# Gate and up products of a SwiGLU MLP with weight columns on the partitions, so that the product needs no transposes

## The reference, cut to what matters

```
h2 = rmsnorm(x, norm_g[l, 1]) * (1.0 + sc2) + sh2
gate, up = jnp.split(h2 @ w_gate_up[l], 2, axis=-1)      # 2048 -> 2 x 5632
x = x + g2 * ((jax.nn.silu(gate) * up) @ w_down[l])      # 5632 -> 2048
```

## Time and profile before

| | |
|---|---|
| median of the runs | 2326.41 us |
| the profiled execution | 2323.81 us, its span 2322.0 us |
| matmuls, each with a load | 9820 |
| of them gate and up products | 4224 (2 layers x 22 chunks x 4 tiles x 24) |
| of them transposes of the MLP | 176 (44 turns x 4) |
| TensorE clock granted, mean | 0.975 of full speed |

### The profile page before, as it was taken

How to read it: one execution, slowest core, us unless ns; L and a number is a source line. 1 busy time by engine, 2 the same in 40 slices (tenths; PEclk the granted TensorE clock), 3 DMA queues, 4 the chain that set the end, 5 groups by cost and what they waited for, 6 DMA issues and landing times.

```text
span 2322.0 us, 26203 instructions
## 1 busy us (share of the span) xinstructions
PE 2158.4 (93%) x9820; PEld 1766.4 (76%) x9820; DVE 1664.1 (72%) x2386; ACT 979.2 (42%) x1400; POOL 202.9 (9%) x388
## 2 busy tenths in 40 slices
PE   2678998689999999999998999998999999999999
PEld 1467786468888888888886877787888888888887
DVE  6977999768867888788786688565975545555555
ACT  3333454154434444443444444445443444444343
POOL 3201111101101111111110011000100000000000
PEclk9889999889999999999998999999999999999999
DMA  9968778748858888888874675443975555555554
GB/s 404 390 241 310 264 273 309 281 154 326 326 191 311 316 321 322 313 317 316 322 304 165 238 294 188 179 166 144 343 280 199 181 196 186 198 182 198 186 195 145
DMA packets 110492, 590.70 MB, mean 254 GB/s; under 512 B 12448, under 2 KB 13088, under 8 KB 63904
## 3 DMA queue, kind: packets, MB, share of 16 engines
q1 hardware_dynamic: 54640, 386.55, 45.6%
q0 software_dynamic: 55296, 201.35, 23.1%
q10 hardware_dynamic: 432, 1.13, 0.1%
HBM read 586.88 MB, written 2.10 MB: 254 GB/s over the span
## 4 chain that ended last, share of the span: by engine, by line
PE 72%; DVE 12%; DMA 9%; issue 5%; ACT 2%; POOL 0%; DVEq 0%; ACTq 0%; POOLq 0%
PE ps L459 22%; PE ps L464 22%; PE ps L463 22%; DMA ada<-w_ada 8%; DVE ada L1202 3%; DVE w_lo L1178 3%; PE ps L762 1%; DMA qT<-w_ada 1%; PE ps L570 1%; PE ps L486 1%; PE ps L659 1%; PE ps L702 1%; PE ps L627 0%; ACT bufa L927 0%; DVE qT L1202 0%
## 5 line engine op out<-in xcount | busy, mean ns | idle before, releaser
L1178 DVE TENSOR_TENSOR w_lo<-raw,w_hi 128x1024 fp32r<-128x1024 f32 x704 | 846.5, 1223 | 366.3 <-ACT w_hi L858 366.0
L858 ACT ACTIVATE w_hi<-raw 128x1024 fp32r<-128x1024 f32 x704 | 734.8, 1057 | 716.0 <-PE ps L464 675.4
L459 PE MATMUL ps<-w_hi,h_hi 128*128 128x512 f32 x1920 | 776.8, 405 | 34.6 <-DVE w_lo L1178 21.6
L464 PE MATMUL ps<-w_hi,h_lo 128*128 128x512 f32 x1920 | 757.6, 395 | 0.0
L463 PE MATMUL ps<-w_lo,h_hi 128*128 128x512 f32 x1920 | 757.6, 395 | 0.0
L459 PEld LDWEIGHTS ps<-w_hi,h_hi 128*128 128x128 f32 x1920 | 367.0, 191 | 118.5 <-issue 33.1
L463 PEld LDWEIGHTS ps<-w_lo,h_hi 128*128 128x128 f32 x1920 | 366.6, 191 | 79.3 <-issue 5.3
L464 PEld LDWEIGHTS ps<-w_hi,h_lo 128*128 128x128 f32 x1920 | 365.9, 191 | 78.4
L459 PE MATMUL ps<-w_hi,a_hi 128*128 128x512 f32 x896 | 356.7, 398 | 5.4 <-issue 2.8
L464 PE MATMUL ps<-w_hi,a_lo 128*128 128x512 f32 x896 | 349.5, 390 | 0.0
L463 PE MATMUL ps<-w_lo,a_hi 128*128 128x512 f32 x896 | 349.1, 390 | 0.0
(11 more groups left out here) (164 smaller groups left out, 1071.3 us busy)
## 6 DMA issues: line engine op xcount, KB each, us to landing
raw<-stream SPq DMA_DIRECT2D x360, 1024.0 KB, 4.9
ada<-w_ada POOLq DMA_DIRECT2D x338, 512.0 KB, 5.7
qT<-w_ada POOLq DMA_DIRECT2D x12, 512.0 KB, 12.0
gate<-w_ada POOLq DMA_DIRECT2D x10, 512.0 KB, 12.5
raw<-stream SPq DMA_DIRECT2D x4, 896.0 KB, 6.7
kT<-w_ada POOLq DMA_DIRECT2D x6, 512.0 KB, 12.0
val<-w_ada POOLq DMA_DIRECT2D x6, 512.0 KB, 10.9
uc<-w_ada POOLq DMA_DIRECT2D x6, 512.0 KB, 12.0
```

What stands on the lines that cost most here:

```text
L459: mm = pe.matmul(bank[:], xh, whi[s][:, k, :], start=begin, stop=False)
L464: mm = pe.matmul(bank[:], xl, whi[s][:, k, :], start=False, stop=end)
L858: act.activation(whi[h % 4][:].rearrange("p k c -> p (k c)"), raw[t % 4][:, a * 1024:(a + 1) * 1024], ACT.Copy).then_inc(hi_ready.sem, 1)
L1178: dve.tensor_tensor(wlo[h % 4][:].rearrange("p k c -> p (k c)"), raw[t % 4][:, a * 1024:(a + 1) * 1024], whi[h % 4][:].rearrange("p k c -> ...
```

## The change

The gate and up products use a new function, `tile_turned`. Here 128 weight columns are loaded and all 256 tokens stream past, so a bank has inner columns on its partitions: bank 0 of a chunk's pair holds the 256 gate columns (two blocks of 128, tokens side by side), bank 1 the up columns. A half tile is 2 sides x 2 blocks x 2 k-steps x 3 matmuls: 24 matmuls with 256 columns, 48 for a tile. silu is one activation of 512 elements per partition, the product with up one operation of 512, and their result already stands as `a_hi` and `a_lo` want it. The transposes, `turned_at` and the MLP's use of banks 5 and 6 go; the down products wait on a new semaphore `ff_ready`. All other products keep `tile`.

```diff
@@ new, beside tile
+            def tile_turned(t, banks, rows, first, last, between=None):
+                h = half_of(t)
+                for a in range(2):
+                    s = (h + a) % 4
+                    pe.wait_ge(hi_ready.sem, hi_ready.at(here, h + a + 1))
+                    pe.wait_ge(lo_ready.sem, lo_ready.at(here, h + a + 1))
+                    for side in range(2):
+                        bank, free, value = banks[side]
+                        if first and a == 0:
+                            pe.wait_ge(free, value)
+                        for i in range(2):
+                            cols = slice((2 * side + i) * P, (2 * side + i + 1) * P)
+                            to = bank[:, i * T:(i + 1) * T]
+                            for k in range(2):
+                                xh, xl = rows[2 * a + k]
...
+                                mm = pe.matmul(to, whi[s][:, k, cols], xh, start=begin, stop=False)
...
+                                pe.matmul(to, whi[s][:, k, cols], xl, start=False, stop=False)
+                                mm = pe.matmul(to, wlo[s][:, k, cols], xh, start=False, stop=end)
+                        mm.then_inc(gemm_done.sem, 1)
+                    if a == 0 and between is not None:
+                        between()
@@ PE, mlp_part
-                def turn(k):
-                    pe.wait_ge(bank_of(k).free.sem, bank_of(k).free.at(here, use(k)))
-                    for tok in range(TOKS):
-                        b = chunk_bank(c0 + k, tok)
-                        pe.wait_ge(chunk_free[b].sem, chunk_free[b].at(here, (c0 + k) // 2 + 1))
-                    for i in range(2):
-                        for tok in range(TOKS):
-                            at = (i * TOKS + tok) * P
-                            src = tok * 256 + i * P
-                            mm = pe.transpose(bank_of(k).tile[:, at:at + P], bufb[:, k % 2, src:src + P], ident)
-                    mm.then_inc(bank_of(k).full.sem, 1)
...
-                    for k in turned_at(o, ups, m):
-                        turn(k)
...
-                    norm(2, t0, (chunk(c0), chunk(c0 + 1)))
+                    norm(2, t0, (chunk(c0), chunk(c0 + 1)), tile_turned)
                 for m in range(8 if o == 0 else 0, 4 * ups):
-                    tile(t0 + m, chunk(c0 + m // 4), h_rows(m % 4), m % 4 == 0, m % 4 == 3, lambda m=m: middle(m))
+                    tile_turned(t0 + m, chunk(c0 + m // 4), h_rows(m % 4), m % 4 == 0, m % 4 == 3,
+                                lambda m=m: middle(m))
...
                     if n == 0:
-                        for k in (2 * g, 2 * g + 1):
-                            pe.wait_ge(bank_of(k).free.sem, bank_of(k).free.at(here, use(k) + 1))
+                        pe.wait_ge(ff_ready.sem, ff_ready.at(here, 6 * o + 2 * g + 2))
@@ ACT, mlp_part
-                        act.activation(bufa[:, k % 2, tok * 256:(tok + 1) * 256],
-                                       ps[chunk_bank(c0 + k, tok)][:, 0:256], ACT.Silu)\
-                            .then_inc(silu_done.sem, 1)
+                    act.activation(bufa[:, k % 2, :], ps[b][:], ACT.Silu).then_inc(chunk_free[b].sem, 1)
...
-                    act.activation(a_hi[:, 2 * k:2 * k + 2, :].rearrange("p k t -> p (k t)"), bank.tile[:],
+                    act.activation(a_hi[:, 2 * k:2 * k + 2, :].rearrange("p k t -> p (k t)"), bufb[:, k % 2, :],
                                    ACT.Copy).then_inc(ff_hi.sem, 1)
@@ DVE, mlp_part
-                        dve.tensor_tensor(bufb[:, k % 2, tok * 256:(tok + 1) * 256],
-                                          bufa[:, k % 2, tok * 256:(tok + 1) * 256], ps[b][:, 256:512],
-                                          ALU.mult).then_inc(chunk_free[b].sem, 1)
+                    dve.tensor_tensor(bufb[:, k % 2, :], bufa[:, k % 2, :], ps[b][:], ALU.mult)\
+                        .then_inc(chunk_free[b].sem, 1)
...
-                    dve.tensor_tensor(a_lo[:, 2 * k:2 * k + 2, :].rearrange("p k t -> p (k t)"), bank.tile[:],
-                                      hi, ALU.subtract).then_inc(bank.free.sem, 1)
+                    dve.tensor_tensor(a_lo[:, 2 * k:2 * k + 2, :].rearrange("p k t -> p (k t)"), bufb[:, k % 2, :],
+                                      hi, ALU.subtract).then_inc(ff_ready.sem, 1)
```

More of the change, by code:

```diff
@@ L87, in done_before @@
     return [m // 4 - 1] if m % 4 == 0 and 1 <= m // 4 <= ups else []
-def turned_at(o, ups, m):
-    return [] if o == 0 and m == 7 else [0, 1] if o == 0 and m == 8 else done_before(o, ups, m)
 def ordered(events):
@@ L121 @@
     + [(50 + j, 0, f"norm2 {j}") for j in range(1, 8, 2)])
-A_MLP, B_MLP = len(A_USE), len(B_USE)
 ST_NORM1, ST_KV, ST_Q0, ST_KCMP, ST_Q1, ST_NORM2, STAGES = 0, 8, 12, 14, 15, 17, 25
@@ L355, in build @@
         squared = count("squared", 16, 0, 8)
-        silu_done = count("silu_done", 12 * PARTS + 2 * LAST_UP, 12)
-        ff_hi = count("ff_hi", 6 * PARTS + LAST_UP, 6)
+        ff_hi, ff_ready = count("ff_hi", 6 * PARTS + LAST_UP, 6), count("ff_ready", 6 * PARTS + LAST_UP, 6)
         cond_ready = count("cond_ready")
@@ L467, in tile @@
                         between()
+            def tile_turned(t, banks, rows, first, last, between=None):
[13 more added lines that the diff above has]
+                                xh, xl = rows[2 * a + k]
+                                begin = first and a == 0 and k == 0 and i == 0
+                                end = last and a == 1 and k == 1 and i == 1
+                                mm = pe.matmul(to, whi[s][:, k, cols], xh, start=begin, stop=False)
+                                if a == 1 and side == 0 and i == 0 and k == 0:
+                                    mm.then_inc(raw_free[t % 4].sem, 1)
+                                pe.matmul(to, whi[s][:, k, cols], xl, start=False, stop=False)
[3 more added lines that the diff above has]
+                        between()
             def h_rows(g):
@@ L488, in norm_turn, with norm @@
                 mm.then_inc(bank.full.sem, 1)
-            def norm(which, t0, chunks):
+            def norm(which, t0, chunks, multiply):
                 split = 8 * (which - 1)
@@ L509, in norm @@
                             pe.wait_ge(h_ready.sem, h_ready.at(here, split + 2 * g + 1))
-                        tile(t, banks, h_rows(g), g == 0, g == 3, between)
+                        multiply(t, banks, h_rows(g), g == 0, g == 3, between)
             def stage_turn(bank, use, st, tok, n, stage=None):
@@ L789, in _ @@
                 here.layer = layer
-                norm(1, T_KV, (chunk(C_KV), chunk(C_KV + 1), window_chunk()))
+                norm(1, T_KV, (chunk(C_KV), chunk(C_KV + 1), window_chunk()), tile)
                 for i, t in enumerate((*T_Q0, *T_Q1)):
@@ L1092, in silu @@
                         act.wait_ge(x_updated.sem, x_updated.at(here, 16 + 8 * o))
[L1093 to L1098, removed]
-                        act.activation(bufa[:, k % 2, tok * 256:(tok + 1) * 256],
-                                       ps[chunk_bank(c0 + k, tok)][:, 0:256], ACT.Silu)\
-                            .then_inc(silu_done.sem, 1)
+                    if k >= 2:
+                        b = chunk_bank(c0 + k, 1)
+                        act.wait_ge(chunk_free[b].sem, chunk_free[b].at(here, (c0 + k - 2) // 2 + 1))
+                    b = chunk_bank(c0 + k, 0)
+                    chunk_done(t0 + (6 if o == 0 and k == 0 else 4 * k + 3), 0)
+                    act.activation(bufa[:, k % 2, :], ps[b][:], ACT.Silu).then_inc(chunk_free[b].sem, 1)
                 def rows(k):
-                    bank, base = (bank_a, A_MLP) if k % 2 == 0 else (bank_b, B_MLP)
-                    act.wait_ge(bank.full.sem, bank.full.at(here, base + 3 * o + k // 2 + 1))
-                    act.activation(a_hi[:, 2 * k:2 * k + 2, :].rearrange("p k t -> p (k t)"), bank.tile[:],
+                    b = chunk_bank(c0 + k, 1)
+                    act.wait_ge(chunk_free[b].sem, chunk_free[b].at(here, (c0 + k) // 2 + 1))
+                    act.activation(a_hi[:, 2 * k:2 * k + 2, :].rearrange("p k t -> p (k t)"), bufb[:, k % 2, :],
                                    ACT.Copy).then_inc(ff_hi.sem, 1)
@@ L1118, in mlp_part @@
                         split_hi(t0 + m + 1, 1)
-                    for k in turned_at(o, ups, m):
+                    for k in done_before(o, ups, m):
                         rows(k)
```

21 lines of the change are left out of this document (8 added, 13 removed).

## The result

The changed kernel takes 2354.07 us (median of four runs, 2348.30 to 2356.98) against 2326.44 us of the kernel before. The ratio is 1.0118, 95% interval 1.0096 to 1.0139: it is slower by some 28 us. The forecast was 2310 us, faster.

A forecast was written before the change was run, and what follows sets the result against it. The MLP was taken as bound by PE's stream of matmuls: +5.7 us for the new pace and -22.2 us for turns and waits gave -16.5 us, so 2310 us, faster, with a range of 2300 to 2339 us.

The forecast's parts named there:

- I take x = 114.0: Gate and up products: x, the pace of a 256-column matmul, is 114.0 ns; 8448 of them add 5.7 us.
- half of p is 113.3 ns: MLP on PE: p, the pace of a 512-column matmul, is 226.7 ns, so one of 256 takes 113.3 ns.
- rival 2: Gate and up products: load and stream no longer absorb each other's delays; 117.7 ns, 2341 us, slower above 116.5 ns; chance 0.22.
- The nearest row: Gate logits, 256 moving tokens and 24 loaded columns: mean 116.0 ns, steady stretch 114.0, taken as the new matmuls' pace.
- The floor by the load: PE in the MLP: a load of 128 columns needs about 111.4 ns, so it fits below 113.3 by some 2 ns.
- Rival 1: Gate and up products: pace is the gate logits' mean, 116.0 ns; +0.3 us, about 2327 us, no change; chance 0.14.
- Rival 3: Gate and up products: loads not hidden behind the stream, or by their 188 ns row; +600 us or more; chance 0.02.
- the turn: MLP on PE: each of the 44 turns removed costs 0.48 us, 21.1 us in all.
- No wait for `ff_ready`: Down products, tightest in the last part: DVE finishes `a_lo` in time, 0.8 us left, so the new wait costs nothing.
- the worth of all turns: MLP on PE: 21.1 us for the turns and 1.1 us of PE's waits go, together 22.2 us.
- what is late next is again PE itself: MLP stretches: with turns gone PE still bounds, since no other engine fills them; the 22.2 us count in full.
- rival 4: PE meets another wait, DVE's low parts in part 0 or `ff_ready`; most of 22.2 us returns, about 2325 us; chance 0.04.

The follow-up runs named there:

- experiment 1: Changed kernel with tile in place of tile_turned in the MLP: tokens loaded, 512 weight columns stream, no turns made; 2311.56 us, ratio 0.9931 to the kernel before.
- experiment 2: Changed kernel with weights loaded but 512 columns of h streaming past each load, half as many matmuls; 2311.38 us, ratio 0.9923 to the kernel before.

## Why the prediction was wrong

**The step that failed** is the pace of the new matmul, "I take x = 114.0". It measured 120.0, which is 8448 x 6.0 = +50.7 us. The whole forecast missed by 44 us (-16.5 forecast, +27.6 by the medians), so this one term more than explains it. Of its three grounds two were wrong.
- The frame: "half of p is 113.3 ns" was taken as the stream's own pace at 256 columns. The 226.7 ns of the earlier trace rows hold 512 columns and one fixed part, and halving halves the fixed part too. Columns at 2.4 GHz take 213.3 of them; the 13.3 left over was in sight. Read as fixed, it gives 106.7 + 13.3 = 120.0, the number measured. One width can't tell a rate from a rate with a constant, so both should have been ends. My upper end was 117.7, and even so the range stopped at 2339 us, 2 below rival 2's own 2341.
- The nearest row: the gate logits match in the moving columns but load 24. The runs with 64, 96 and 128 loaded go at 113.3, 116.0 and 120.0, so at 256 the load's size matters, and the row was near in the wrong dimension. "Loading as such doesn't slow the stream" rested on it and is wrong at 256.
- The floor by the load, 111.4 ns, was right (111.6 with fp32r), and beside the point.

**Rival 2** had the side right (slower, "above x = 116.5") and the size too small (117.7 ns, 2341 us). Its mechanism, delays in load and stream that a matmul of 512 still absorbs and one of 256 doesn't, isn't what the runs show: the pace is even, and the same 13.3 ns stand at 512. That the load takes part at 256 (113.3 ns with 64 loaded) it had right in part. Rival 1 (116.0) fell. Rival 3's ways, loads in series or by their row of 188 ns, fell again: the load rows are 192 ns long and start every 120.

**Right**: the turn, 0.48 us (experiment 1, and the downs, 65.31 us for the 65.3 forecast). No wait for `ff_ready`: at the last part's end the downs start and DVE finishes as follows.

```profile
1191.29 0.40 PE L449 MATMUL ps<-w_hi,a_hi 128*128 128x512 f32 x1
```

```profile
1191.59 0.69 DVE L1549 TENSOR_TENSOR bufb<-bufa,ps 128x512 f32<-128x512 f32 x1 [2.34 <-PE ps L484]
1192.20 2.35 DVE L1174 TENSOR_TENSOR w_lo<-raw,w_hi 128x1024 fp32r<-128x1024 f32 x2
1194.47 0.68 DVE L1555 TENSOR_TENSOR a_lo<-bufb,a_hi 128x512 fp32r<-128x512 f32 x1
```

`a_lo` is there at 1195.15, against 1181.13 - 1176.45 = 4.68 us behind the downs' start expected, 3.86 now, and needed after 24 x 0.227 = 5.4. The wide operations take what was taken for them, DVE's product 687 ns (0.69), ACT's silu 600 (0.60) and its copy 618 (0.63):

```profile
L1549 DVE TENSOR_TENSOR bufb<-bufa,ps x44: 679/687/689, 522.9 to 2305.6; 128x512 f32<-128x512 f32 x44
```

**Half right**: the worth of all turns. With the pace kept (experiment 1) the kernel gains 16 us, not 22.2, because "what is late next is again PE itself" doesn't hold in part 0: there it is a transfer of the conditioning matrix, with DVE's low part behind it. I had read the stretches of parts 1 and later and the normalisation, not the rest of part 0, though the 2.3 us of the earlier trace rows all lie in the two parts 0 (1.1 and 1.3 us), where DVE was late already. So rival 4's wait in part 0 was real. At 114.0 it would have taken some 6 us of the gain, the 12 turns of 0.48; that is an estimate from experiment 1, whose stream is nearly as fast.

Summed by part: parts 1 to 3 of layer 0 grow from 531.41 to 1236.31 - 692.06 = 544.25 us, +12.84; of 3072 x 6.67 - 16 x 0.48 that is +12.8. Layer 1 has the same +12.85 (529.70 to 542.55). The parts 0 grow by 5.1 and 2.4 us (229.45 to 234.55, 224.54 to 226.90) where the arithmetic for PE alone gives 4.8 each. Together that is +33.2 us; the profiled executions differ by 32.4.

## What to carry to other kernels

A pace read at one matmul width is a rate plus a constant. Before the number of matmuls changes at equal columns, take it apart (the clock's N / 2.4 and the rest) and charge the rest once per matmul with its load: 13.3 ns for fp32r with 128 loaded columns. By that sum 4224 extra ones cost 56 us here, of which 48 showed. Keep 512 columns per matmul where an operand swap allows it, since the swap itself was free at 512 (experiment 2); and look for the nearest row in every dimension of the operation, the loaded one too.

## What was unexpected of the hardware

- 64 loaded columns with 512 moving go slower (230.0 ns) than 128 with 512 (226.7), and 64 x 384 pays twice the fixed part of 64 x 256. Not explained.
- The kernel with 128 moving columns ran part 0 of both layers at about half clock. From 462 us in layer 0, and from 1628 us in layer 1:

```profile
462.00:625.00 163.00, 152.20 (x697) 149.03 (x698) 77.01 (x115) 51.29 (x70) 7.91 (x15) 0.52 0.41 145
625.00:700.00 75.00, 75.00 (x508) 73.49 (x507) 51.78 (x67) 24.14 (x26) 10.54 (x20) 0.76 0.74 273
767.60:896.10 128.50, 128.50 (x1153) 128.50 (x1151) 103.63 (x127) 55.28 (x59) 16.43 (x32) 1.00 0.86 319
...
1545.00:1628.00 83.00, 83.00 (x387) 66.65 (x386) 56.67 (x81) 38.20 (x63) 0.00 (x0) 1.00 0.46 169
1628.00:1800.00 172.00, 163.82 (x763) 161.16 (x761) 77.27 (x113) 53.32 (x71) 8.45 (x16) 0.53 0.39 141
```

The granted clock (before the last two numbers of a row) is 0.52 there, near the level of 1.2 GHz, with starts 213 or 214 ns apart for most; then 0.76, and 1.00 for the same matmuls in part 1. In layer 1 it is 1.00 from 1545 to 1628 us with PE busy all the time, and 0.53 from then on with PE busy for 163.82 of 172 us. The kernel with 192 moving columns was granted 0.94 from 462 to 625 us, the changed kernel 0.96. The two parts 0 up to their down products took 238.9 and 234.3 us, against 163.0 and 155.3 with 192 moving columns. These 155 us are why the kernel took 2452.85 us and the one with 192 took 2298.71, with the same 111.6 ns in part 1. What tipped the clock isn't shown.
